# Half-norm waits for the projections, and weight splits placed further ahead in the merge and the down projection

## The reference

```python
# first block, layer i (mixers left out)
u_lat = modulate(h_lat, g_pre_mix[i], ml[0], ml[1])        # norm m0 (i = 0), m1 (i = 1); then u @ w_in
...
h_lat = h_lat + ml[2] * rms_norm(o_lat, g_post_mix[i])
f_lat = sqrelu_mlp(modulate(h_lat, g_pre_ff[i], ml[3], ml[4]), w_ff1[i], w_ff2[i])   # norm f0, f1; then u @ w1
...
# second block
h = rms_norm_2(x, norm_mix_w)                              # norm m2
proj = h @ w_in
...
x = x + (gate_a * y_a + gate_b * y_b) @ w_mix_out          # the merge
h = rms_norm_2(x, norm_ffn_w)                              # norm u
u = causal_dwconv(h @ w_ffn_up, ffn_conv_w, ffn_conv_b)
u_gate, u_val = jnp.split(u, 2, axis=-1)
x = x + (silu(u_gate) * u_val) @ w_ffn_down                # the down projection
return rms_norm_2(x, norm_final_w)
```

## Time and profile before

| | us |
|---|---|
| median of 3 runs | 1964.32 (1961.51 to 1964.5) |
| the profiled execution | 1967.42 |
| its span in the profile | 1965.4 |
| PE busy | 1815.0 |
| mean granted TensorE clock | 0.959 |

### The profile page before, as it was taken

How to read it: one execution, slowest core, us unless ns; L and a number is a source line. 1 busy time by engine, 2 the same in 40 slices (tenths; PEclk the granted TensorE clock), 3 DMA queues, 4 the chain that set the end, 5 groups by cost and what they waited for, 6 DMA issues and landing times.

```text
span 1965.4 us, 39348 instructions
## 1 busy us (share of the span) xinstructions
PE 1815.0 (92%) x16690; PEld 1503.2 (76%) x16690; DVE 1106.5 (56%) x1632; ACT 870.1 (44%) x1376; POOL 221.3 (11%) x220
## 2 busy tenths in 40 slices
PE   4999898998898899999998999899989999979998
PEld 2866677877777688888887777798878776769996
DVE  4357755565455644324536766665456476657874
ACT  4136544353342543314425356465332266546652
POOL 0000035434263000000001100000000000000210
PEclk8999988999998999999999999899989999989999
DMA  8342152223231322323223520365545633335553
GB/s 284 116 151 65 46 180 89 89 96 102 72 105 66 109 81 89 104 90 100 93 91 82 152 74 23 109 192 176 190 138 156 206 104 106 129 128 172 186 169 117
DMA packets 201660, 237.14 MB, mean 121 GB/s; under 512 B 14379, under 2 KB 158605, under 8 KB 201485
## 3 DMA queue, kind: packets, MB, share of 16 engines
q1 hardware_dynamic: 196555, 227.52, 36.6%
q10 hardware_dynamic: 4930, 7.11, 1.1%
HBM read 233.56 MB, written 1.05 MB: 119 GB/s over the span
## 4 chain that ended last, share of the span: by engine, by line
PE 76%; DVE 11%; ACT 6%; issue 2%; DMA 2%; POOL 1%; SPq 1%; ACTq 1%; DVEq 0%; POOLq 0%
PE bank L1644 18%; PE bank L1645 17%; PE bank L1646 17%; PE bank L1840 10%; DVE window L2147 3%; ACT window L2740 2%; PE bank L1695 2%; PE bank L1828 2%; DMA arena<-in_w_ada 2%; PE bank L1807 2%; PE bank L1819 1%; PE bank L1847 1%; PE bank L1811 1%; PE bank L2025 1%; DVE arena L2481 1%
## 5 line engine op out<-in xcount | busy, mean ns | idle before, releaser
L1646 PE MATMUL bank<-window 128*128 128x512 f32 (+1 forms) x1980 | 686.4, 347 | 0.0
L1645 PE MATMUL bank<-window 128*128 128x512 f32 (+1 forms) x1904 | 675.6, 355 | 0.0
L1644 PE MATMUL bank<-window 128*128 128x512 f32 (+1 forms) x1732 | 623.2, 360 | 32.2 <-DVE window L2147 8.6
L1646 PEld LDWEIGHTS bank<-window 128*128 128x128 f32 x1980 | 384.4, 194 | 45.6
L1644 PEld LDWEIGHTS bank<-window 128*128 128x128 f32 x1732 | 337.0, 195 | 90.4 <-DVE window L2147 13.2
L1645 PEld LDWEIGHTS bank<-window 128*128 128x128 f32 x1904 | 370.8, 195 | 46.0 <-issue 0.5
L2147 DVE TENSOR_TENSOR window<-arena,window 128x2048 fp32r<-128x2048 f32 (+1 forms) x132 | 297.1, 2250 | 186.4 <-ACT window L2740 184.5
L2740 ACT ACTIVATE window<-arena 128x2048 fp32r<-128x2048 f32 (+2 forms) x252 | 310.8, 1233 | 175.4 <-DMA arena<-in_w_ff 50.9
L2740 ACT ACTIVATE arena<-bank 128x256 f32<-128x256 f32 (+1 forms) x264 | 114.5, 434 | 333.3 <-PE bank L1646 110.8
L1840 PEld LDWEIGHTS bank<-arena 64*64 64x64 f32 x5888 | 206.2, 140 | 34.6 <-ACT arena L2740 11.1
L1840 PE MATMUL bank<-arena 64*64 64x64 f32 (+1 forms) x5888 | 219.3, 231 | 12.7 <-ACT arena L2740 4.7
(11 more groups left out here) (296 smaller groups left out, 2034.2 us busy)
## 6 DMA issues: line engine op xcount, KB each, us to landing
arena<-in_w_ff SPq DMA_DIRECT2D x64, 1024.0 KB, 5.4
arena<-in_w_ada SPq DMA_DIRECT2D x48, 1024.0 KB, 5.8
arena<-in_w_in SPq DMA_DIRECT2D x23, 1024.0 KB, 5.2
arena<-in_w_ffn_up SPq DMA_DIRECT2D x22, 1024.0 KB, 5.1
arena<-in_w_ffn_down SPq DMA_DIRECT2D x10, 1024.0 KB, 5.1
arena<-in_w_in_even SPq DMA_DIRECT2D x9, 1024.0 KB, 5.5
arena<-in_w_out SPq DMA_DIRECT2D x8, 1024.0 KB, 5.3
arena<-in_w_in_odd SPq DMA_DIRECT2D x8, 1024.0 KB, 5.5
```

The lines of the kernel that those rows point to most:

```text
L1644: e.matmul(o, rr(l[0]), rr(r[0]), start=start, stop=False)
L1645: e.matmul(o, rr(l[0]), rr(r[1]), start=False, stop=False)
L1646: return e.matmul(o, rr(l[1]), rr(r[0]), start=False, stop=stop)
```

## The change

Three edits.

1. `fm` and `fm_half` wait first only for every second point (q = 0), and for the others (q = 4) before the fifth chunk k. The first gates of the second block wait in each call only for the half (y) that they read.
2. In the merge, a position for a split is kept behind the steps of both columns of y = 0, not only of the first. Another is kept after the loads of y = 1 instead of between the matmuls of m = 0 and m = 1 of y = 1, and "root table" moves behind it. Read through the plan: the split of chunk (c 1, y 1) moves from behind "root table" to ahead of z turn 2. The split of `up` chunk 1 moves from behind the scaled rows of norm u, block 0, to right behind the split of `up` chunk 0. "Root table" goes behind both.
3. In the down projection a position is kept behind the last matmuls of c = 0. The split of chunk (c 1, y 1) moves from behind "root table" to ahead of the spread of the final gain, and no other split moves.

```diff
@@ -536,7 +536,7 @@
             if c == 0:
-                if name == "mix1":
+                if name in ("mix1", "down"):
                     early.append((len(plan), False))
                 run(*beside)
@@ -1542,14 +1542,14 @@
         cols(("mix2", c, 0), W_m, c * 512, 512, 0, 4)
         for m in range(2):
             step("mix2", c, 0, m)
-        if not c:
-            early.append((len(plan), False))
+        early.append((len(plan), False))
     z_turn(2)
     z_turn(3)
     run(spread_(("gain u",)))
-    step("root table")
     for c in range(2):
         cols(("mix2", c, 1), W_m, c * 512, 512, 4, 4)
+    early.append((len(plan), False))
+    step("root table")
     for m in range(2):
         for c in range(2):
             step("mix2", c, 1, m)
@@ -1647,8 +1646,10 @@
         def fm(w, f0, x, s, u, *points, last=False):
 
-            pe.wait_ge(w.ready, u.before, *points)
+            pe.wait_ge(w.ready, u.before, *points[0::2])
             for k in range(w.nk):
+                if k == 4:
+                    pe.wait_ge(*points[1::2])
                 i = split_product(u.b[:, s], [a[:, k, f0:f0 + 128] for a in (w.v.hi, w.v.lo)], [a[:, k, s] for a in (x.hi, x.lo)],
                                   k == 0, k == w.nk - 1)
@@ -1666,8 +1667,10 @@
                 w, f0 = ws[f // 2], f % 2 * 128
-                pe.wait_ge(w.ready, us[f].before, *points[4 * h:4 * h + 4])
+                pe.wait_ge(w.ready, us[f].before, *points[4 * h:4 * h + 4:2])
                 for k in range(8):
+                    if k == 4:
+                        pe.wait_ge(*points[4 * h + 1:4 * h + 4:2])
@@ -2050,7 +2053,7 @@
-            wide(chunks[nm, j, y], X, 4 * y, k, bank(nm, j, k), y == 0, y == 1, *second_x[2 * k:2 * k + 2], last=k == 1)
+            wide(chunks[nm, j, y], X, 4 * y, k, bank(nm, j, k), y == 0, y == 1, second_x[2 * k + y], last=k == 1)
```

## The result

The changed kernel takes 1940.08 us in the median of 4 runs (1938.86 to 1942.63), the kernel before 1964.41 beside it (4 runs). The ratio is 0.9884 [0.9869, 0.9899]: 24.3 us less. Four more runs of the changed kernel, in a later series, gave 1942.14 us and a ratio of 0.9894 [0.9877, 0.9910]. The forecast was 1943.6 and 20.7 us.

The account below looks back on a forecast made before the run. PE, busy 1815.0 of 1965.4 us, was taken as the bound. Waits 9.9 - 0.1, merge 3.8, down 3.5, clock 1.4 + 2.2 sum to 20.7 us: 1943.6 from 1964.32; likeliest 1939 to 1946 (0.50), 8-in-10 range 1937 to 1951.

Parts of the forecast that it names:

- m0: Edit 1, norm m0: twelve matmuls fit into PE's gap of 2.61 us, gaining 2.5 us.
- f0: Edit 1, norm f0: first wait gains 0, block 3's transposes already waiting for DVE; second wait gains 1.3 us.
- m1: Edit 1, norm m1: two waits gain 1.3 us each, the chain moving along with PE; together 2.5 us.
- f1: Edit 1, norm f1: PE restarts after the q = 0 part, at 1252.70 instead of 1254.15, gaining 1.4 us.
- m2: Edit 1, norm m2: two restarts each gain one DVE operation, the second following from the first; 1.4 us.
- u: Edit 1, norm u: one restart gains 0.8 us, as ACT's second rounding already delays q = 4 a little.
- merge: Edit 2: the 2.58 us stall goes and up 1's subtraction leaves the chain to norm u, gaining 3.8 us.
- down: Edit 3, down projection: the whole 3.54 us stall for chunk (c 1, y 1) goes, gaining 3.5 us.
- Rival D: Stalls are handed on to later waits at most places, leaving 8 to 9 us, time 1956; chance 0.06.
- The clock: Low-clock spells behind stalls: the down projection's goes, 1.4 us, and one or two of seven others, 2.2 us.
- rival F: Most low-clock spells go, so the clock gives much: 26 to 31 us, time 1933 to 1938; chance 0.10.
- rival E: Merge: up 1's weights land late, its rounding holds ACT's queue and norm u, making the kernel slower; chance 0.02.

Follow-up runs that it names:

- f0_split_later: Changed kernel with the weight split ahead of block 2's values in norm f0 moved behind the values; 1939.15 us, in a repeat 1935.66.
- both_ahead: Changed kernel with the moves of heads_ahead and f0_split_later together; 1946.37 us, ratio 0.9908 against the kernel before.
- mask_and_f0_later: f0_split_later with POOL's mask additions in layer m1 also made to wait for DVE's third scaling; 1942.42 us, ratio 0.9898 against the kernel before.
- after_again: The changed kernel run once more, unaltered, in a later series; 1942.14 us, ratio 0.9894 against the kernel before.
- waits_only: The kernel before with edit 1 alone, the half-norm waits; 1951.43 us against 1963.82, ratio 0.9935.
- merge_only: The kernel before with edit 2 alone, the merge; 1958.15 us against 1963.82, ratio 0.9976.
- down_only: The kernel before with edit 3 alone, the down projection; 1956.92 us against 1963.82, ratio 0.9961.
- merge_c1y1_only: The kernel before with only edit 2's first half, the split of (c 1, y 1) ahead of the z turns; 1961.74 us against 1963.82, ratio 0.999.
- heads_ahead: Changed kernel with the second chunk behind each norm's output projection split ahead of the last column's matmuls; 1948.97 us, ratio 0.9921 against the kernel before.
- mask_later: Changed kernel with POOL's two mask additions in layer m1 made to wait for DVE's third scaling; 1944.87 us against 1963.26, ratio 0.9909.

## Why the prediction was right, point by point

**The stalls.** The likeliest case was 1939 to 1946; the kernel took 1940.08 and 1942.14. The stall terms made 17.1 us and measured 16.6. m0 2.5 (2.6), f0 1.3 (0.4), m1 2.5 (2.6), f1 1.4 (1.4), m2 1.4 (1.46), u 0.8 (0.85), merge 3.8 (3.84), down 3.5 (3.5). These are differences of idle time; by the starts of the matmuls m0 and the down projection give 2.9 and 3.7. The heading of edit 1 says seven waits and its list has nine restarts, which changes no sum. The price of a wait in the middle of 24 matmuls, 0.1, is not to be seen: f1 gives 1.38 where 1.45 lay between the q = 0 part and the restart. The Trainium skill (TensorE: Matmul & The Clock Gate, "Architectural detail") says that PE pulls weight loads ahead of matmuls in flight, and a wait in mid-projection could keep it from that, which the prediction bounded at 1.6 us from rows. The traces show nothing of that size.

**f0.** "0" for the first wait was right, and why: f0_split_later takes the split out of the chain, and 3.2 us appear. "1.3" for the second wait was mis-sized: a low stretch now lies over the transposes, behind the longer stall, and 0.4 was left. In the four traces with the later split (f0_split_later and its repeat, both_ahead, mask_and_f0_later) the stall is 0.6 us, the stretch is gone and the second wait gives 1.3. The prediction counted that stall as idle time in which nothing is lost, and a longer stall has a price of its own in the matmuls behind it.

**Stalls handed on.** Rival D at a small size: beside f0, m1's transposes wait 1.21 us at block 3, and PE's wait behind the scalings of layer m1 grew by 1.6. The first of these is small: in after_again and waits_only the wait is absent and PE runs at half clock there instead, and from m1's first restart to these transposes it is 11.2 us with the low stretch and 11.0 with the wait. The prediction said that m1's chain moves along with PE, which held up to there. It did not follow the lead on to a chain that starts from a landing and from POOL.

**The clock.** This term was too small by the mean clocks: 3.6 us (1.4 + 2.2). A run's mean granted clock and its time go together: a straight line through all 127 runs of the eleven kernels with more than one run, with one slope for all and a level for each kernel, makes a run 1.04 us longer for each 0.001 of mean clock that is missing (what is left scatters by 1.7 us). At equal clock the changed kernel is 16.6 us ahead of the one before (give or take some 1.5), and its mean clock is 0.9698 (8 runs) against 0.9640 (52), which gives another 6.0. The single edits come out the same way: 8.4, 4.0 and 4.9 at equal clock, 17.3 together. So the time won by removing stalls is what the traces say, and the clock adds some 6.0, not 3.6, in the direction of rival F and short of its 9.4 to 13.4.

The traces show where part of it is. The 1.4 for the down stretch was right. Of the seven other stretches, for which the prediction took one or two to go and 2.2 us, two go and pay in every trace with edit 1: those behind the second restarts of f0 and m1. From 706.6 to 715.0 of before it takes 8.2 us in the four traces without edit 1 (before, merge_only, down_only, merge_c1y1_only) and 6.7 in the nine with it, and from 1075.2 to 1085.0 9.9 to 10.0 and 8.4: 1.5 us each. The table by stretches, first the kernel before behind f0, then the changed kernel there, then after_again behind m1, where the kernel before has 0.50:

```profile
708.00:710.00 2.00, 2.00 (x12) 2.00 (x11) 0.00 (x0) 0.00 (x0) 0.00 (x0) 0.50 0.00 0
...
703.00:705.00 2.00, 2.00 (x19) 2.00 (x18) 0.00 (x0) 0.60 (x1) 0.00 (x0) 1.00 0.00 0
...
1064.00:1065.00 1.00, 1.00 (x6) 0.82 (x5) 0.35 (x1) 0.00 (x0) 0.00 (x0) 1.00 0.64 98
```

The one behind f0's first restart goes as well and its time is handed on, the one behind m1's first goes in some executions and is worth 0.3, and m2's two stay. That makes 4.4 us at named places, less the 0.9 over f0's transposes: close to the 3.6 of the prediction. The rest of the 6.0 has no place. Low stretches elsewhere differ between the two traces, as at 85 to 89, where PE runs at half clock before and at full clock after. But merge_only, whose program is the same as before's up to there, has none either, so this one is the spread between executions and not shown to be a gain of the change. What decides whether such a stretch falls in an execution is open: after_again has one at 1046 that its twin has not.

**Edit 2 and rival E.** The landing of `up` 1 was late by 0.81 us for ACT and cost nothing. heads_ahead shows what the mechanism costs when the weights are not there: 8 to 9 us, 4.5 of them at equal clock.

## What to carry to other kernels

A wait for all parts of an operand can be split into one before the first matmul and one before the first matmul that reads the rest; it pays one operation of the engine that makes the parts, at each place where the next chain starts from PE, and nothing where it does not. Moving a weight split ahead pays as long as the weights have landed by then: ACT runs its queue in order, and a rounding that waits for a landing holds all the norm's steps behind it. Where PE's clock has two levels, compare kernels at equal mean clock before explaining a difference of a few us, and compare one trace with several of the other kernel before giving a low stretch to the change. What an edit gives by the clock itself, like the 1.4 us of the down projection, is not in the difference at equal clock.

## What the runs showed of the hardware that I had not expected

**A POOL addition holds a DVE operation with two inputs in SBUF until it ends.** In the trace of before the scaling of 128x256 values on DVE (L2555) runs four times: it takes 485 ns in the shortest and 4677 ns in the longest case, from 1103.60 to 1108.28, while POOL's addition runs from 1102.95 for 5.05. The line of the source in the trace of before (ns: shortest, median, longest):

```profile
L2555 DVE SCALAR_TENSOR_TENSOR arena<-arena x5: 485/485/4677, 1102.8 to 1129.2; 128x256 f32<-128x256 f32 x4, 128x512 f32<-128x512 f32 x1
```

Which DVE operations are held shows in mask_later: those with both inputs in SBUF (arena and arena, arena and window) are, those with an input from a bank (0.42 at 1104.48, 0.69 at 1103.76) are not, and neither are the reciprocals with their single input (6.93 for three, with POOL beside them or without). POOL is held in turn: its two additions take 11.10 us beside DVE's subtraction in mask_later and 9.55 in the changed kernel. The Trainium skill states this rule (SBUF — State Buffer, "Who interferes with whom"): whichever engine starts first has the shared ports for the whole instruction. The traces agree. A held operation is shown as busy and not as waiting, so no list of waits has it; the sign is one instance far longer than the others of its line.

**The stalls that I followed often have a low stretch behind them, but not always.** The stall of 3.5 us in the down projection brought one in every trace that has it. Behind the one of 2.58 in the merge the kernel before has none, and waits_only, with the same stall at 1734.94, has one at 1736 to 1740. A low stretch costs 1.3 to 1.5 us at these places, where PE is the bound, and the longer one of waits_only in the down projection 2.8 (8.59 us from the restart in place of 5.83). The kernel before alone spreads over 1957.96 to 1966.24 us in one series of 11 runs.
